# Two decoder blocks: the latents of mla are normed inside the fox stage, and mla opens with its queries

## The reference, cut to what matters

```python
def rmsnorm(x, gain):
    xf = x.astype(jnp.float32)
    y = xf * lax.rsqrt(jnp.mean(xf * xf, axis=-1, keepdims=True) + NORM_EPS)
    return (y * gain.astype(jnp.float32)).astype(x.dtype)
...
    log_f = jax.nn.log_sigmoid(fox_f.astype(f32) + fox_b_f.astype(f32))
    fox_out = block_causal_attention(fox_q.reshape(fox_shape), fox_k.reshape(fox_shape),
                                     fox_v.reshape(fox_shape), FOX_HEAD_DIM ** -0.5,
                                     jnp.cumsum(log_f, axis=1))
...
    q = (rmsnorm(mla_cq, mla_q_norm) @ mla_w_uq).reshape(b, s, MLA_HEADS, MLA_QK_DIM)
    q_nope, q_rope = jnp.split(q, [MLA_NOPE_DIM], axis=-1)
    kv = (rmsnorm(mla_ckv, mla_kv_norm) @ mla_w_ukv).reshape(b, s, MLA_HEADS, MLA_NOPE_DIM + MLA_V_DIM)
    k_nope, mla_v = jnp.split(kv, [MLA_NOPE_DIM], axis=-1)
...
    mla_out = block_causal_attention(q_full, k_full, mla_v, MLA_QK_DIM ** -0.5)
```

## Time and profile before

| what | value |
|---|---|
| median of the runs | 2951.28 us (2949.66 to 2953.05) |
| the profiled execution | 2948.04 us, its span 2945.5 us |
| TensorE (matmul) busy | 2680.8 us, 91% of the span |
| VectorE busy | 1861.6 us, 63% |
| ScalarE busy | 1365.9 us, 46% |
| DMA | mean 131 GB/s |
| mean granted clock of TensorE | 0.944 of full speed |

### The profile page before, as it was taken

How to read it: one execution, slowest core, us unless ns; L and a number is a source line. 1 busy time by engine, 2 the same in 40 slices (tenths; PEclk the granted TensorE clock), 3 DMA queues, 4 the chain that set the end, 5 groups by cost and what they waited for, 6 DMA issues and landing times. The chain is left out here.

```text
span 2945.5 us, 58188 instructions
## 1 busy us (share of the span) xinstructions
PE 2680.8 (91%) x25276; PEld 2287.0 (78%) x25276; DVE 1861.6 (63%) x2628; ACT 1365.9 (46%) x1929; POOL 83.7 (3%) x120
## 2 busy tenths in 40 slices
PE   7989779999898689999998897899999988978999
PEld 6777658898777578888887764788888877747888
DVE  5656767956757678846575444666565655346664
ACT  5524346656433266644463232654444542326543
POOL 0010000000110000000001100000000011000000
PEclk9998989999999899999998897999999988879999
DMA  5311224554202144635532120345555422203453
GB/s 221 115 47 71 72 88 173 202 206 171 103 30 87 58 158 172 221 142 201 189 142 71 69 72 31 142 174 203 197 204 188 150 76 70 75 29 129 173 201 127
DMA packets 54686, 386.57 MB, mean 131 GB/s; under 512 B 6688, under 2 KB 7328, under 8 KB 8352
## 3 DMA queue, kind: packets, MB, share of 16 engines
q1 hardware_dynamic: 54432, 382.86, 36.2%
HBM read 381.79 MB, written 1.05 MB: 130 GB/s over the span
## 5 line engine op out<-in xcount | busy, mean ns | idle before, releaser
L336 PE MATMUL banks<-normed_high,weights_high 128*128 128x256 f16 (+1 forms) x4096 | 1141.9, 279 | 42.4 <-DVE weights_low L322 19.9
L337 PE MATMUL banks<-normed_low,weights_high 128*128 128x256 f16 (+1 forms) x4096 | 1141.1, 279 | 0.0
L338 PE MATMUL banks<-normed_high,weights_low 128*128 128x256 f16 (+1 forms) x4096 | 1139.8, 278 | 0.0
L322 DVE SCALAR_TENSOR_TENSOR weights_low<-weight_ring,weights_high 128x2048 f16<-128x2048 f32 x336 | 765.4, 2279 | 371.3 <-ACT weights_high L316 356.0
L316 ACT ACTIVATE weights_high<-weight_ring 128x2048 f16<-128x2048 f32 x306 | 580.6, 1898 | 222.3 <-PE banks L338 209.7
L336 PEld LDWEIGHTS banks<-normed_high,weights_high 128*128 128x128 f16 (+1 forms) x4096 | 409.6, 100 | 120.1 <-issue 29.6
L336 PE MATMUL banks<-projected,weights_high 128*128 128x256 f16 x1696 | 465.4, 274 | 29.3 <-DVE projected L347 29.3
L337 PE MATMUL banks<-projected,weights_high 128*128 128x256 f16 x1696 | 465.6, 275 | 0.0
L338 PE MATMUL banks<-projected,weights_low 128*128 128x256 f16 x1696 | 465.4, 274 | 0.0
L338 PEld LDWEIGHTS banks<-normed_high,weights_low 128*128 128x128 f16 (+1 forms) x4096 | 408.9, 100 | 55.9
L337 PEld LDWEIGHTS banks<-normed_low,weights_high 128*128 128x128 f16 (+1 forms) x4096 | 408.5, 100 | 55.4 <-issue 1.3
(11 more groups left out here) (401 smaller groups left out, 2914.7 us busy)
## 6 DMA issues: line engine op xcount, KB each, us to landing
weight_ring<-w SPq DMA_DIRECT2D x356, 1024.0 KB, 4.8
small_weights<-small SPq DMA_DIRECT2D x2, 1280.0 KB, 8.0
constants<-const SPq DMA_DIRECT2D x1, 1697.0 KB, 10.3
weight_ring<-w SPq DMA_DIRECT2D x2, 640.0 KB, 3.8
residual<-xt SPq DMA_DIRECT2D x1, 1024.0 KB, 5.0
small_weights<-small SPq DMA_DIRECT2D x2, 512.0 KB, 10.8
out<-residual SPq DMA_DIRECT2D x4, 256.0 KB, 2.3
parameters<-par SPq DMA_DIRECT2D x2, 115.5 KB, 9.8
```

The source lines that it names most:

```text
L322: nc.vector.scalar_tensor_tensor(out=self.part(self.mem.w_low, g), in0=self.part(self.mem.ring, g), scalar=W_SCALE, in1=self.part(self.mem ...
L336: pe.matmul(out, w_high, high, start=start, stop=False, skip_group_check=skip)
L337: pe.matmul(out, w_high, low, start=False, stop=False, skip_group_check=skip)
L338: return pe.matmul(out, w_low, high, start=False, stop=stop, skip_group_check=skip)
```

## The change

A class `Latents` takes the norm of the latents out of mla and puts it, in pieces, into fox: the squares behind `f_size` on VectorE; the sums behind the turned values on TensorE, into the banks 5 and 6 in place of 0 and 1; the means between the first two `gates.low`; the roots on ScalarE behind `gates.high` of the second block; the reciprocal and the three scaled tiles on VectorE behind step 2 of the attention. The units of fox write the banks 5 and 6 (the products with the values), so TensorE now waits for `mean_squares` before the first unit. The buffers of the squares and roots lie in columns 32 x 256 to 37 x 256 of `scratch`. Mla drops all of these, and its TensorE list begins with the queries. The number of instructions on TensorE is the same. On ScalarE one table load for each layer goes: before, Sqrt and then Exp were loaded in mla; now Sqrt and Exp are loaded in fox, and mla finds Exp there.

```diff
-    def vector(self, dve, nc, sig, link, say, lows):
+    def vector(self, dve, nc, sig, link, say, lows, beside={}):
...
             if i in lows:
                 self.gates.low(dve, nc, sig, lows[i])
+            for step in beside.get(i, ()):
+                step()
...
+class Latents:
+
+    def __init__(self, nc, mem, sig):
+        self.nc, self.mem, self.sig = nc, mem, sig
+        cut = Cutter(mem.beside_gates[:, 32 * 256:])
+        self.sq, self.rstd = cut(3, T), cut(2, T)
+        self.c_all = mem.proj[:, X_CQ:X_CKV + 1, :]
+
+    def squares(self, link, say, need):
+        say(self.nc.vector.tensor_tensor(self.sq, self.c_all, self.c_all, ALU.mult), "squares")
+
+    def sums(self, pe, need):
+        need("squares", 1)
+        for i in range(3):
+            mm = pe.matmul(self.mem.ps[:, 5 + i // 2, 0:T], self.mem.c("ones"), self.sq[:, i, :],
+                           start=(i != 1), stop=(i != 0))
+        mm.then_inc(self.sig("square_sums"), 1)
+
+    def means(self, link, say, need):
+        V, rstd, ps = self.nc.vector, self.rstd, self.mem.ps
+        need("square_sums", 1)
+        link(V.tensor_scalar(rstd[:, 0, :], ps[:, 5, 0:T], 1.0 / 256, EPS, ALU.mult, ALU.add))
+        say(V.tensor_scalar(rstd[:, 1, :], ps[:, 6, 0:T], 1.0 / 128, EPS, ALU.mult, ALU.add),
+            "mean_squares")
+
+    def roots(self, say, need):
+        need("mean_squares", 1)
+        say(self.nc.scalar.activation(self.rstd, self.rstd, ACT.Sqrt), "roots")
+
+    def normed(self, link, need):
+        V, rstd = self.nc.vector, self.rstd
+        need("roots", 1)
+        link(V.reciprocal(rstd, rstd))
+        for i in range(3):
+            g = C2["q_norm"] + i
+            link(V.scalar_tensor_tensor(out=self.c_all[:, i, :], in0=self.c_all[:, i, :],
+                                        scalar=self.mem.par[:, g:g + 1], in1=rstd[:, i // 2, :],
+                                        op0=ALU.mult, op1=ALU.mult))
...
 def fox_stage(nc, mem, sig, gates):
...
                 "f_size")
+            latents.squares(link, say, need)
             need("values_turned", 1)
...
             gates.low(dve, nc, sig, 0)
+            latents.means(link, say, need)
             gates.low(dve, nc, sig, 1)
-            att.vector(dve, nc, sig, link, say, {4: 2, 7: 3})
+            att.vector(dve, nc, sig, link, say, {4: 2, 7: 3},
+                       {2: [lambda: latents.normed(link, need)]})
...
             gates.high(act, nc, sig, 1)
+            latents.roots(say, need)
             att.scalar(act, nc, sig, say)
...
             mm.then_inc(sig("values_turned"), 1)
+            latents.sums(pe, lambda name, n: pe.wait_ge(sig(name), n))
             pe.wait_ge(sig("values"), 1)
             pe.wait_ge(sig("forget_sums"), 1)
+            pe.wait_ge(sig("mean_squares"), 1)
             att.tensor(pe, sig)
...
 def mla_stage(nc, mem, sig, gates):
...
-            need("squares", 1)
-            for i in range(3):
-                mm = pe.matmul(ps[:, i // 2, 0:T], mem.c("ones"), sq[:, i, :],
-                               start=(i != 1), stop=(i != 0))
-            mm.then_inc(sig("square_sums"), 1)
-            need("latents", 3)
             for h in range(HEADS):
                 for k in range(2):
                     mm = pe.matmul(tiles(0, HEADS)[0:W, h, :], w_uq[:, k, h * W:(h + 1) * W],
                                    c_all[:, k, :], start=(k == 0), stop=(k == 1))
```

More of the change, by code:

```diff
@@ L2334, in fox_stage @@
                     scale=HD ** -0.5, bias=add_bias, gates=gates)
+    latents = Latents(nc, mem, sig)
     with nc.Block() as block:
@@ L2390, in mla_stage @@
     qf, kf, vt = cut(HEADS, T), cut(HEADS, T), cut(NBLK, MIX)
-    sq, rstd = cut(3, T), cut(2, T)
     ps, par = mem.ps, mem.par
@@ L2413, in _ @@
             V = nc.vector
-            say(V.tensor_tensor(sq, c_all, c_all, ALU.mult), "squares")
             gates.low(dve, nc, sig, 0)
-            need("square_sums", 1)
-            link(V.tensor_scalar(rstd[:, 0, :], ps[:, 0, 0:T], 1.0 / 256, EPS, ALU.mult, ALU.add))
-            say(V.tensor_scalar(rstd[:, 1, :], ps[:, 1, 0:T], 1.0 / 128, EPS, ALU.mult, ALU.add),
-                "mean_squares")
-            need("roots", 1)
-            link(V.reciprocal(rstd, rstd))
-            for i in range(3):
-                g = C2["q_norm"] + i
-                say(V.scalar_tensor_tensor(out=c_all[:, i, :], in0=c_all[:, i, :],
-                                           scalar=par[:, g:g + 1], in1=rstd[:, i // 2, :],
-                                           op0=ALU.mult, op1=ALU.mult), "latents")
             need("queries_out", 1)
@@ L2446, in _ @@
             gates.high(act, nc, sig, 0)
-            need("mean_squares", 1)
-            say(nc.scalar.activation(rstd, rstd, ACT.Sqrt), "roots")
             need("queries_summed", 1)
```

## The result

| what | before | after |
|---|---|---|
| median of the runs | 2950.47 us (2947.24 to 2953.05, 4 runs) | 2925.78 us (2921.77 to 2931.61, 4 runs) |
| ratio, 95% interval | | 0.9924 [0.9905, 0.9942] |
| the profiled execution, its span | 2948.04 us, 2945.5 us | 2924.72 us, 2922.8 us |
| mean granted clock of TensorE | 0.944 | 0.949 |

The change is faster by about 22 us (by the ratio; its interval is 17 to 28 us). The waits that were forecast came out in size; the clock did not.

What follows compares the result with a forecast made beforehand. TensorE, busy 91% of the span, was taken as the bound. Per layer 10.83 - 2.63 - 2.24 = 5.96 us, 11.9 for two, plus 0.9 of clock: 12.8 us off the median 2951.28 gives 2938.5 us, range 2931.5 to 2947.

Steps and rivals of the forecast that it cites:

- What goes in mla: In mla, the queries have only the barrier ahead of them and start 10.83 us earlier in each layer.
- Squares and sums: In fox, squares (0.96 us) fit VectorE's 1.11 us wait for Ln, sums (2.11 us) fit TensorE's idling; cost 0.
- The wait for the means: In fox, TensorE's first scores wait for the means, so the first gate tile starts 2.63 us later.
- Exp's table: On ScalarE in fox, loaded behind the root by 1727.1, before VectorE's first maximum at 1727.4; cost 0.
- Reciprocal and scaled tiles: On VectorE in fox, 4.96 us, of which a gate tile covers 2.73; TensorE waits 2.24 us at its third turn.
- more than once: Sign of being wrong: TensorE in fox waiting for scaled probabilities at more than the single forecast place.
- The clock: TensorE's clock after its idle times move: queries could gain up to 4.35 us, fox lose 1.6; net 0.9 us gain.
- half of each: Halving the possible clock gain of the queries and loss in fox: + 2.2 - 1.3 = 0.9 us.
- rival B: Queries at full clock (4.35 us) and first layer's swap as fast as the second's (3.4): 19.6 us gain; chance 0.14.
- C: Fox gives most back, both its costs showing whole: 4.6 us gain in all, 2946.7 us; chance 0.21.
- D: Gaps of 3.6 and 2.24 us in fox keep TensorE at 1.2 GHz: 8 us slower, 2959 us; chance 0.06.

Runs made afterwards that it cites:

- fox's part alone: Fox as in the changed kernel, mla keeping its whole chain but writing the normed tiles to an unread buffer; 2954.7 us, ratio 1.0017 to the kernel before.
- no norm at all: The kernel before with the norm of the latents left out of mla and nothing added to fox; 2921.58 us, ratio 0.9902.
- the version with no waits in fox: Changed kernel, TensorE's wait for the means moved to the first product with the values, norm's VectorE work cut in three; 2925.77 us, ratio 0.9917.
- the changed kernel with matmuls added: Changed kernel plus unread matmuls: 6 behind the turned values, 20 behind the sums, 14 behind the queries of mla; 2928.45 us, ratio 0.9921.
- 128x256 added: Changed kernel with one unread VectorE operation of that size (about 0.4 us) at the head of fox; one run, 2929.72 us.

## Why the predicted gain was too small, step by step

**What goes in mla: right.** The idling ahead of the queries is 1.84 us where 1.75 was expected, the queries start 10.8 us nearer to fox's end, and the copy on ScalarE waits for the queries (5.26 us) and starts as soon as they end.

**Squares and sums: right.** The squares have taken the cover: 0.47 us of the 1.11 us wait for the Ln are left. The sums took 2.93 us, since the clock was low, and ended 3.9 us ahead of the scores.

**The wait for the means: right in size.** The first gate tile starts 10.1 us behind the first turned value, 2.36 us later; I had 2.63.

**Exp's table: right in cost, wrong in order.** I had it loaded by 1727.1, ahead of the first maximum. It is loaded behind that maximum, at 1731.44, and the first exponential waits the 1.28 us for it; TensorE is busy 10.00 us from 1730.10 to 1740.10 all the same.

**Reciprocal and scaled tiles: right in size.** 2.04 us in both layers; I had 2.24.

**A second wait for scaled probabilities: missed.** The last turns wait 0.56 us in each layer. I had named "more than once" as a sign of being wrong. It is small, and it goes with the clock: over all profiles it is there in each of the 12 layers whose last 5 us of fox are at the full level, and in none where they are all at the low level.

So the waits that were forecast make 2 x (10.83 - 2.36 - 2.04) = 12.9 us in place of 11.9.

**The clock: this step failed.** I took "half of each", + 2.2 - 1.3 = 0.9 us. The two stretches became 14.3 + 12.6 = 26.9 us shorter. Taking the 12.9 us of waits off leaves 14.0 us to the clock, by subtraction, where I had 0.9. The queries gave 2.34 + 1.94 = 4.3 us: all of rival B's 4.35, not half. The swap gave nothing, 1.7 us in the first layer and the same lost in the second. Fox gave the rest: with its two waits it should have ended 65.3 + 4.4 = 69.7 and 67.5 + 4.4 = 71.9 us behind its start, and ended at 65.9 and 66.0, so 3.8 + 5.9 = 9.7 us (the two waits of 0.56 us are already taken off). I had weighed the clock of fox only as a loss, and had no term for the low level late in fox, though I had read it: its slices from 1760 to 1780 us are at 1.00 in the kernel after. The first layer's fox begins 3.65 us later than before, though no part of the change lies ahead of it; with 1.75 us lost between the layers and 1.2 won behind them, 26.9 becomes 22.7 us, which is the difference of the spans.

**How much of this is luck.** The queries' share has a cause in the change, the shorter idling. Fox's share has none that was shown: with the same instructions up to the end of fox, the first body was 62.1 us in fox's part alone and 55.8 us here. In the profiled execution that is a matter of how fox met the clock. The miss itself is not the luck of one execution: the changed kernel's two sets of runs, 4 and 6, have the ratios 0.9924 and 0.9928.

By whole runs instead of one profile: mla's side was worth 26 to 29 us (from fox's part alone to the changed kernel, and no norm at all) where I had 21.7, and fox's side cost 5 to 8 us (fox's part alone; changed against no norm, (0.9928 - 0.9902) x 2950 = 7.7) where I had 9.7. The waits came out as forecast, so what is left of both errors is put down to the clock; both have the same sign. Of the rivals B was the nearest, with 19.6 us; its mechanism came half true (the queries yes, the swap no), and its size came from fox. C and D did not come true here. The bodies of 62.1 and 64.7 us show that fox's clock can indeed cost 6 to 9 us in a layer against 55.8 us, but not that the gaps bring it down, as D had it.

The Trainium skill (TensorE: Matmul & The Clock Gate, HAM oscillation) says that gaps between bursts bring the clock down and the next burst starts slow. For the hole of mla the trace agrees: filling it took the queries from 9.46 to 7.07 us. By the same rule the version with no waits in fox should have no worse a clock there than the others; it had 0.86 and 0.82, the changed kernel with 4.4 us of waits 0.95, and fox's part alone fell to 0.61 with TensorE busy 10.00 of the 10.00 us ahead. The measurement decides: inside fox gaps alone do not set the level.

**What stays open.** What fixes the place of the falls. Three profiles of the changed program agree in every body from starts 8 us apart, while fox's part alone, the same program up to there, started between them and had another pattern. So the start counted from the start of the trace is not the place that counts. The traces do show another place that goes with the bodies: how long the clock has been up when fox starts. The stretch before the last rise ahead of fox and the stretch from that rise to fox's first matmul, for the kernel after:

```profile
1701.60:1704.90 3.30, 3.30 (x18) 2.33 (x16) 2.82 (x6) 0.21 (x1) 0.00 (x0) 0.50 0.00 0
1704.90:1720.10 15.20, 13.90 (x127) 12.28 (x126) 2.09 (x2) 2.33 (x7) 0.00 (x0) 1.00 0.20 70
```

and for fox's part alone:

```profile
1702.40:1705.70 3.30, 3.30 (x16) 2.38 (x17) 2.24 (x4) 0.21 (x1) 0.00 (x0) 0.50 0.00 0
1705.70:1721.90 16.20, 14.89 (x137) 13.18 (x136) 3.90 (x5) 2.36 (x7) 0.00 (x0) 1.00 0.19 66
```

Fox's first layer starts 15.2 us behind the rise in all three profiles of the changed kernel, with a body of 55.7 us. It starts 16.2 us behind it in fox's part alone, in the changed kernel with matmuls added and in the one with 128x256 added, and all three have 62.1 us. With the fox of the kernel before, the three layers that start 16.2 to 16.4 us behind the rise have 57.5 us, and the four at 14.9 to 15.0 us have 59.7. It is not the whole answer: in the second layer the changed kernel's 55.9 us came three times at 14.8 us, and fox's part alone had 59.4 at 14.9, where 128x256 added had 55.8. No run varied this distance alone, and why an execution arrives at 15.2 or at 16.2 us is open.

## What to carry to other kernels

Removing a stall ahead of float32 matmuls is worth the stall and the clock that the stall took from the work behind it; price that work at the full level if idling is nearly all gone (22 of 28 layers here). Where TensorE is busy throughout at a mean clock of 0.82 to 0.86, a few microseconds of waits more or less are not what its time hangs on: widen the range by the spread of that stage (here 3 to 5 us in a layer to either side), and measure several versions that differ by a shift before an edit is called good. A profile whose fast stage is the same twice is no proof: repeat the stage in a program that differs only behind it, as fox's part alone did here.

## What the runs showed of the hardware

- One list of instructions in one stage took 54.4 to 59.8 us, or with a wait 55.7 to 64.7 us, at granted clocks of 0.79 to 0.95. The slow pieces come in the midst of full work too (0.61 behind ten microseconds busy 10.00 of 10.00).
- Over seven programs each, the mean body is 59.2 us with the wait of 2 us and 58.2 us without it. The layers of each group spread over 6 to 9 us, so this difference of 1.0 us is told neither from nothing nor from the wait's whole length.
- The same 16 passes of the swap took 3.69, 5.38 or 7.07 us and never anything between, whatever stood ahead of them.
